# Three stages of a block become one stage walked by quarters of the sequence

## The reference

```python
h = x @ w_in + b_in                        # 1024 -> 9 groups of 512 columns
q_a, k_a, v_a, g_a, q_h, z_fwd, z_bwd, i_h, g_h = split(h)
# 8 heads of 64: tokens form 32 rows of 64; a token sees 8 rows x 16 columns around it
o_a = neighbourhood_attention(q_a, k_a, v_a, rpb) * silu(g_a)
# 4 heads of 128, forwards and backwards over the tokens
f = lb + (1 - lb) * sigmoid(z);  k = 1 - f
S_t = diag(f_t) S_{t-1} + k_t outer i_t;   o_t = S_t^T q_t
o_h = rms_norm(o_fwd + o_bwd) * gain * silu(g_h)
y = concat(o_a, o_h) @ w_out + b_out
return layer_norm(2**0.25 * x + y)
```

## Time and profile before

| | us |
|---|---|
| median of 3 runs (5614.87 to 5622.78) | 5621.27 |
| the profiled execution | 5620.12 |
| its span, first to last instruction | 5618.3 |
| block 3: turning and splitting x to the first projection matmul | 3613 to 3645 |
| block 3: projections | 3645 to 4437 |
| block 3: attention and recurrence | 4437 to 5343 |
| block 3: loading `w_out`, output projection and normalisation | 5343 to 5618 |

### The profile page before, as it was taken

The page is one execution under the profiler, slowest core; times in us unless marked ns, Lnnn a source line. Parts: engine busy times, 40 slices in busy tenths (PEclk is TensorE's granted clock), DMA queues, the critical chain, the costliest instruction groups (busy, mean ns, idle before and its releaser), DMA issues. The chain is left out here.

```text
span 5618.3 us, 61740 instructions
## 1 busy us (share of the span) xinstructions
PE 4567.0 (81%) x25432; PEld 3642.6 (65%) x25432; DVE 2463.2 (44%) x3040; ACT 1651.1 (29%) x2678; POOL 977.9 (17%) x529
## 2 busy tenths in 40 slices
PE   5999999988996999946766627799999866777767
PEld 2788888886775778824545515688888844555556
DVE  3488788625554303242222232211110177776733
ACT  2111111125554112212212224433331044545522
POOL 1111111112221111101101124211111032222123
PEclk9999999998997999968888858899999978888888
DMA  4111111232333111137766641322222243242132
GB/s 160 49 42 57 53 57 42 92 115 86 113 113 111 38 68 57 53 130 192 208 197 184 183 176 55 138 92 92 92 93 72 62 97 90 71 106 66 44 131 92
DMA packets 505640, 557.31 MB, mean 99 GB/s; under 512 B 45963, under 2 KB 396495, under 8 KB 498385
## 3 DMA queue, kind: packets, MB, share of 16 engines
q1 hardware_dynamic: 427409, 412.18, 24.7%
q10 hardware_dynamic: 77954, 141.19, 7.1%
HBM read 343.50 MB, written 193.00 MB: 95 GB/s over the span
## 5 line engine op out<-in xcount | busy, mean ns | idle before, releaser
L226 PE MATMUL ps<-hh,wsplit 128*128 128x512 f32 x2944 | 1173.8, 399 | 29.7 <-issue 25.1
L227 PE MATMUL ps<-hl,wsplit 128*128 128x512 f32 x2944 | 1164.9, 396 | 0.0
L228 PE MATMUL ps<-hh,wsplit 128*128 128x512 f32 x2944 | 1162.1, 395 | 0.0
L812 DVE SCALAR_TENSOR_TENSOR conv_acc<-conv_in,pcol,conv_acc 128x1024 f32<-128x1024 f32 x480 | 687.5, 1432 | 14.8
L226 PEld LDWEIGHTS ps<-hh,wsplit 128*128 128x128 f32 x2944 | 556.4, 189 | 161.6 <-issue 34.3
L218 POOL TENSOR_TENSOR wsplit<-wraw,wsplit 128x1024 fp32r<-128x1024 f32 x108 | 300.4, 2791 | 2023.0 <-ACT wsplit L213 2023.0
L227 PEld LDWEIGHTS ps<-hl,wsplit 128*128 128x128 f32 x2944 | 561.1, 191 | 131.5 <-issue 3.9
L228 PEld LDWEIGHTS ps<-hh,wsplit 128*128 128x128 f32 x2944 | 558.0, 190 | 127.8
L251 PE MATMUL ps<-wo,o_yh 128*128 128x512 f32 x1024 | 418.8, 409 | 79.6 <-DVE o_yl L2940 64.4
L252 PE MATMUL ps<-wo,o_yh 128*128 128x512 f32 x1024 | 413.3, 404 | 0.0
L253 PE MATMUL ps<-wo,o_yl 128*128 128x512 f32 x1024 | 411.5, 402 | 0.0
(11 more groups left out here) (305 smaller groups left out, 7039.1 us busy)
## 6 DMA issues: line engine op xcount, KB each, us to landing
wraw<-in_w_in SPq DMA_DIRECT2D x108, 512.0 KB, 3.9
sh<-hy_ak ACTq DMA_DIRECT2D x64, 512.0 KB, 4.7
o_ld<-y_tiles SPq DMA_DIRECT2D x48, 512.0 KB, 5.3
g_tiles<-b_ost SPq DMA_DIRECT2D x96, 256.0 KB, 2.4
wo_raw<-in_w_out SPq DMA_DIRECT2D x32, 512.0 KB, 5.0
x_rows<-o_x ACTq DMA_DIRECT2D x32, 512.0 KB, 2.6
hy_dec<-in_k_dec SPq DMA_DIRECT2D x64, 256.0 KB, 3.0
hy_kt<-sh SPq DMA_DIRECT2D x32, 512.0 KB, 6.7
```

The costliest lines, as they stand in the source:

```text
L226: e.matmul(p[:, :], wh, c.HH[tb][:, k, :], start=k == 0, stop=False)
L227: e.matmul(p[:, :], wh, c.HL[tb][:, k, :], start=False, stop=False)
L228: t = e.matmul(p[:, :], wl, c.HH[tb][:, k, :], start=False, stop=k == 7)
L812: e.scalar_tensor_tensor(v, a[:, h * 1024 + j:(h + 1) * 1024 + j], c.convw(j, ch), v, ALU.mult, ALU.add) \
```

## The change

One stage, `b3_*`, takes the place of the three.

- The tokens are walked in four quarters (`tb`) of 36 slots each, 144 in all. Each quarter turns and splits its own 512 tokens of x into one `L.HH`, `L.HL` (8x512 each), and loads and splits all 36 column tiles again: 144 loads and splits instead of 36, in a ring of four.
- Between slots the list places the recurrence, now in 64 units of 256 tokens whose inputs (k, b, f - b, q, values) stay in SBUF, and the attention.
- The recurrence's forward direction is finished in place. The backward direction runs from the last token, which is not known yet, so only its part within a chunk is made in the slots; its q factors and key-value products are stored to DRAM. After slot 144, 16 `chain` steps walk the states backwards, add them to the stored outputs, and normalise (`fin`, `fin2`, two heads at a time).
- An attention step now takes 4 rows by 16 columns of queries against up to 12 rows by 32 columns of keys: 384 keys, or 256 for the first and the last 4 rows. There are still 128 steps: 0, 16, 32 and 32 of them in the four quarters, and 48 after slot 144.
- The output projection begins at slot 163 of the same list, two slots to a tile, while attention steps are still placed until slot 178. Tiles go in the order `L.seq`. The bias is now added by GpSimd ahead of the statistics.
- Loads and stores are all issued by SP. Matmuls of projections and outputs share two PSUM banks, attention two, and products, key-value products and outputs of the recurrence one each; before, each stage had three to eight.
- Copies out of PSUM that ScalarE made before (queries and keys, L2146; turned keys, L2545) are made by VectorE.

The core of the diff (`b3_order` gives the places; the engine programs follow it):

```diff
-def p3_layout(c):
-    L = c.p3 = K()
...
-def mix_layout(c):
-    L = c.mx = K()
...
-def o3_layout(c):
-    L = c.o3 = K()
...
+    o = al(8192)
+    L.W, L.Wraw = view("w3", o, 4, 2048, r=True), view("w3_raw", o, 4, 2048)
+    o = al(8192)
+    L.HH, L.HL = view("h3_hi", o, 8, 512, r=True), view("h3_lo", o + 4096, 8, 512, r=True)
...
+    L.pb, L.ab = Banks(c, c.P[0:2]), Banks(c, c.P[2:4])
+    L.ra, L.rb, L.ob = Banks(c, c.P[5:6]), Banks(c, c.P[6:7]), Banks(c, c.P[7:8])
...
+def b3_order(L):
...
+    for tb in range(4):
+        for q in range(2):
+            pair("i", q, 28 + 2 * q)
+        for hd in range(4):
+            col("f", (hd, 0), 20 + hd)
+            col("f", (hd, 1), 24 + hd)
+            rq[tb, hd] = len(slots)
+            col("rq", hd, 16 + hd)
+            if tb < 3:
+                for kind, column in (("rg", 32), ("ag", 12), ("aq", 0), ("ak", 4)):
+                    col(kind, hd, column + hd)
...
+        if n >= 4:
+            after(last[n - 4], "ld", n)
+            before(last[n - 4] + 2, "split", n)
...
+    for n, (tb, hd, d, h) in enumerate(L.units):
+        r = rq[tb, hd]
+        e = r + (1, 2, 4, 5)[2 * d + h]
+        if d == 0 and h == 0:
+            before(r, "log", tb, hd)
+        before(e, "el", n)
+        after(e + 2, "prod", n)
+        after(e + 3, "state", n)
+        after(e + 4, "out", n)
...
+    def att_at(m, s):
+        v, a, j = L.steps[m]
+        after(s, "qk", m)
+        before(s + 1, "div", m)
+        after(s + 1, "turn", m)
+        after(s + 2, "val", m)
...
+        if g == 0:
+            s = 36 + 3 + 2 * k
+        elif g < 3:
+            s = 36 * (g + 1) + 3 + k
+        else:
+            s = 147 + k // 2 if g == 3 else 155 + 2 * k // 3
...
+    t0 = 144
+    for k in range(8):
+        after(t0 + k // 4, "wo", k)
+    for q, tb in enumerate(range(3, -1, -1)):
+        for hd in range(4):
+            n, s = 4 * q + hd, t0 + 1 + 4 * q + hd
+            after(s - 2 if n >= 2 else s, "ch_ld", n)
+            after(s - 2 if n in (2, 3) else s if n < 2 else t0 + 4 * q - 4 + (hd | 1) + 5, "fin_ld", n)
+            after(s + 1, "chain", n)
+            after(s + 2, "ch_o", n)
+            after(s + 3, "fin", n)
+            if n % 2:
+                after(s + 4, "fin2", n)
+    o0 = t0 + 19
+    L.seq = [15, 14] + list(range(9, -1, -1)) + [13, 12, 11, 10]
+    after(o0 - 2, "o_const")
+    for i in range(16):
+        s = o0 + 2 * i
+        after(s - 4, "y_ld", i)
+        before(s - 2, "y_split", i)
+        after(s, "o", i, 0)
+        after(s + 1, "o", i, 1)
+        after(s + 2, "o_end", i)
...
+def b3_sp(e, c):
...
+    def ld(n):
+        if n >= 4:
+            e.wait_ge(*L.done[L.last_unit[n - 4]])
+        col = tile_col(L, n)
+        e.dma_start(L.Wraw[:, n % 4, 1024:2048].rearrange("p (k n) -> p k n", k=8), w_in[:, col:col + 128].rearrange("(k p) n -> p k n", p=128)) \
+            .then_inc(*L.w_ld[n % 4].up(n))
...
+        for g in range(g0, g1 + 1):
+            for j in range(4):
+                src = c.VA[256 * g:256 * (g + 1), cs].rearrange("(r x) n -> r x n", x=64)[:, COL0[j]:COL0[j] + 32, :]
+                e.dma_start(L.V[:, s, 4 * (g - g0) + j, :], src).then_inc(*L.v_ld[s].up((v, g, j)))
...
+        elif k == "fin_ld":
+            n = s[1]
+            tb, hd = chain_unit(n)
+            sl = slice(512 * tb, 512 * tb + 512)
+            if n >= 4:
+                e.wait_ge(*L.ry_st[n % 4][n - 4])
...
+            e.dma_start(L.FO[n % 4], L.OD[hd][:, sl]).then_inc(*L.fo_ld[n % 4].up((n, "o")))
...
+def b3_pool(e, c):
...
+        elif k == "o" and s[2] == 1:
+            i = s[1]
+            e.wait_ge(*c.by_dve["out", 3, i, 1])
+            e.wait_ge(*L.c3_ld["ln_bias_3"])
+            e.tensor_tensor(L.XO[:, i % 3, :], L.XO[:, i % 3, :], L.bo, ALU.add).then_inc(*L.o_pool.up(("bias", i)))
+        elif k == "o_end":
+            i = s[1]
+            X = L.XO[:, i % 3, :]
+            e.wait_ge(*L.o_dve["n", i])
+            e.tensor_tensor(X, X, L.lg, ALU.mult).then_inc(*L.o_pool.up(("g", i)))
+            e.wait_ge(*L.o_pool["g", i])
+            e.tensor_tensor(X, X, L.lb, ALU.add).then_inc(*L.o_pool.up(("y", i)))
```

More of the change, by code:

```diff
@@ L2017, in b2_done @@
     return [L.o_pe[15, 1], L.o_act[("rs", 15), 1], c.by_dve["out", 2, 15, 1], L.o_pool[15], L.x2_st[0][14], L.x2_st[1][15]]
-def p3_layout(c):
-    L = c.p3 = K()
[L2024 to L2062, removed]
-    L.bound_a, L.bound_d = sig("bound_by_act"), sig("bound_by_dve")
-    L.f_out = [[dsig(f"forget_out{i}{j}") for j in range(3)] for i in range(2)]
-    L.f_log, L.f_step = sig("forget_log"), sig("forget_step")
@@ new lines, in tile_col, with levels, v3 @@
+def tile_col(L, n):
+    return L.tiles[n][2] * 128
+def levels(L, n):
+    tb, hd, d, h_ = L.units[n]
+    s, out = n % 2, []
+    for B, X in ((128, L.X[0]), (64, L.X[1]), (32, L.X[2])):
+        h = B // 2
+        qs, ks = (slice(h, B), slice(0, h)) if d == 0 else (slice(0, h), slice(h, B))
+        x = v3(X[:, s, :], B)
+        kd = x if B > 32 else v3(L.K32[d][:, s, :], 32)
+        out.append((B, x, kd, qs, ks))
+    return out
+def v3(v, m):
+    return v.rearrange("p (n x) -> p n x", x=m)
@@ new lines, in rq_unit, with chunk_unit, chain_state @@
+def rq_unit(L, tb, hd):
+    return next(u for u in L.order if u[0] == "col" and u[2:5] == (tb, "rq", hd))
+def chunk_unit(hd, at):
+    return first_of(at // 4, hd) + at % 4 // 2
+def chain_state(e, c, n, tb, hd):
+    L = c.b3
+    e.wait_ge(*L.ch_ld[n % 2][n, "kv"])
+    if n == 0:
+        e.wait_ge(*L.r_pe[63, "out", 1])
+        for q in L.qe_st:
+            e.wait_ge(*q.end())
+    for m in range(4):
+        j, k = 3 - m, 4 * (n // 4) + m
+        to, now, kv = chain_slot(L, hd, k + 1), chain_slot(L, hd, k), L.KC[:, n % 2, (3 - m) * 128:(4 - m) * 128]
+        if k == 0:
+            e.tensor_copy(to, kv).then_inc(*L.ch_dve.up((n, 1)))
+        else:
+            e.wait_ge(*state_in(L, n, m))
+            e.scalar_tensor_tensor(to, now, L.decb[:, 4 * tb + hd, j:j + 1], kv, ALU.mult, ALU.add).then_inc(*L.ch_dve.up((n, (m + 1) % 4)))
@@ new lines, in values @@
+    def values(m):
+        v, a, j = L.steps[m]
+        pr, groups, g0, g1 = L.visits[v]
+        w = L.avs.index((v, a))
+        bs, gs = step_bias(L, m)
+        e.wait_ge(*c.by_act["turn", m])
+        if j == 0 and w:
+            e.wait_ge(*c.by_dve["att_o", w - 1])
+        if m == L.first_step[v]:
+            e.wait_ge(*L.v_ld[v % 2][v, g1, 3])
+        for hh in range(2):
+            for i, g in enumerate(gs):
+                o = 256 * (w % 2) + 64 * j
+                t = e.matmul(c.P[4][64 * hh:64 * hh + 64, o:o + 64], L.V[:, v % 2, 4 * (g - g0) + j, 64 * hh:64 * hh + 64],
+                             L.PT[:, m % 3, 128 * i + 64 * hh:128 * i + 64 * hh + 64], start=i == 0, stop=i == len(gs) - 1)
+        t.then_inc(*L.a_pe.up(("val", m)))
@@ L2994, in o3_pe, with value_unit @@
                      L.WO, h, before if h == 0 else None).then_inc(*L.o_pe.up((i, h)))
+def value_unit(L, tb, hd, t):
+    return next(u for u in L.order if u[0] == "row" and u[2:] == (tb, "i", hd // 2, t))
 def sp_program(e, c):
```

1727 lines of the change are left out of this document (914 added, 813 removed).

## The result

The changed kernel takes 5640.57 us, median of 20 runs (5619.26 to 5662.54), against 5622.9 us of the kernel before in the same rounds: ratio 1.0033, 95% interval 1.0021 to 1.0044. It is a third of a per cent slower. The forecast was 5340 us.

A forecast was written before the change was run, and what follows sets the result against it. PE was taken to bound the slots: 3635 start + 1133 work + 113 order + 36 turning = 4917; plus 182 to the outputs and 240 for them, 5339, with 1.8 of profile excess 5341, said as 5340; range 5205 to 5550.

The forecast's parts named there:

- The slots: Block 3's projection slots with recurrence and attention beside them: PE is the bound, 1133 us of work, ending at 4917.
- their tenth: In the slots: engines walking in order cost 10% on top of PE's work, 113 us, between bounds of 7 and 317.
- the prediction's last rival: ScalarE's table loads in block 3: 2.66 us each with a drain, 57 more switches 152 us instead of 73; no chance of its own.
- the slower rival: In the slots: weight loads through SP's in-order list set the pace, slower than before from 10.6 us a slot, 5680; chance 0.08.
- the order bound for the slots: In the slots: the engines' order costs 317 us instead of 113, as in the mixed stage before, 5545 us; chance 0.22.
- all covered: From slots to outputs: waits nearly all hidden, slots pay 7, the part to 163 takes 150, outputs 228: 5190; chance 0.10.
- Slots 144 to 163: Between the projection slots and the outputs: 22 us of exposed load plus 160 for 16 slots, 182 us, bounds 134 and 214.
- exposed `w_out`: After the last projection slot: loading and splitting the output weights takes 28 us, of which 22 remain exposed.
- The output tiles: Output projection at the end: 114 us with attention, 111 without and a last chain of 15: 240 us, between 225 and 270.
- So tiles alone go at 11.65: Output tiles without attention: POOL's bias, statistics to gain, and gain and shift set 11.65 us a tile, 9.5 tiles 111 us.
- With attention ... I take 17.5 with waits: Output tiles beside attention: 16.7 us of PE work, 17.5 with waits, 6.5 tiles 114 us.
- The forecast's paragraph on the lock: In the slots: DVE and POOL block each other at a shared port, DVE gains 30 to 65 us, the sum unchanged.

## Why the prediction was wrong, by its own steps

**The slots: right.** 4917 forecast, 4916.5 measured; the first projection matmul at 3623.7 instead of 3635, so 11 us more went between them, and two misses cancel in the end point. Without the turning (13.3 to 13.9 us between quarters, 12 forecast) the quarters take 281, 292, 340 and 341 us, where the forecast's terms with their tenth give 275, 294, 337 and 337. The order cost of 10% holds in sum (1252.5 us for 1133 of work). It doesn't hold for each part: a step of the attention costs 2.3 us there, a quarter over its 1.85 and not a tenth. ACT loads its tables 190 times in block 3, exactly as counted, and a switch costs 1.31 us from the end of one operation to the start of the next (median of the kernel's 341), so the dearer price of the prediction's last rival is not paid here. ACT is busy 193 and 194 us in the last two quarters, where some 220 were reckoned, and DVE 220 and 227, where it was 200. ACT did stand 94.6 us for weight loads in all, but a slot came to 9.0 us, 9.5 in the last two quarters, below the 10.6 at which the slower rival would have decided. That rival, the order bound for the slots, and "all covered" all fell.

**Slots 144 to 163: the step that failed first.** "Between 7 and 12 us a slot I take 10: 160." Measured: (304.5 - 29.1) / 16 = 17.2 us, outside both bounds. The exposed `w_out` (22 us) was about right; the floor of the whole is 29.1. The mistake was the overlap: a slot was priced as one fin step with the attention beside it, 8.55 us, but the chain alone takes 8.2 us a slot and the attention alone 7.4, and the two add up (131 + 118.5) instead of overlapping. The store and load of the normalised rows were counted as the rows' median (2.4 + 3.4 us) without SP's place for them; they take 4.7 and some 4.5 to 5.0 here, and 25 us more come from SP's order. The forecast looked at DVE's work, "about 6 us in each" slot, and DVE was indeed busy 102 of 303 us.

**The output tiles: the larger error, 157 us.** "So tiles alone go at 11.65": POOL's own loop was walked, SP's list was not. In it stands the store of tile i-3, which waits for POOL, ahead of the load of tile i. With that one place changed, tiles take 12.0 us, so POOL's loop was about right and SP's, which stood above it, was missing. Only the last seven tiles pay it in full, since the first two had been loaded ahead (11.2 and 13.2 us): from 5455.0, the first matmul of the first tile alone, to the end of the last matmul the nine tiles take 140 us, where 9.5 at 11.65 were 111. The end behind them takes 22 us and not 15. "With attention ... I take 17.5 with waits": they took 36 ((5454.1 - 5237.7) / 6). From the first output matmul to 5455.0 that is 234 us and not 114, 120 us of the miss and the larger part; the order of load and normalisation takes 7 us a tile back (29.2), gain and shift off POOL 1.7. The forecast priced those tiles by PE's work, 11.2 + 3 x 1.85; the 117.7 us by which O falls without the attention are three times what that formula allows for 20 steps (20 x 1.85 = 37). What fills the rest of such a tile is not shown. The forecast's paragraph on the lock concluded that it changes nothing in the sum, and with the order mended no price of it can be told from nothing.

**The other side.** The rival that was to end slower sat in the slots. The one that happened, a tail of 48 attention steps and 16 chain steps with nothing large to hide them, was in the forecast's list only as a range of 134 to 214 us, which can't reach the other side.

**Left open.** What a step's 5 us in the tail consist of. PE's busy time in S is 115.6 us at a mean clock of 0.63. If all of it had run at the lower level, half the full clock, the full clock would have saved at most half of it; so by this estimate the clock explains at most 58 of the 275 us. The rest is waits from engine to engine and for transfers, which no run here took apart. DMA was half busy in S (0.50, 146 GB/s), and transfers do slow each other there: the stores of the normalised rows land in 4.7 us beside the attention and in 2.4 and 2.7 without it. For the eight pairs of heads that is some 2 us each, an estimate from these landings, and small beside 275. Issuing V from POOL was not tried.

## What to carry to other kernels

Work that fits into the shadow of a large stage costs little more than its PE time there (2.3 us a step against 1.85), and outside it cost more than twice that (5.5 us): count the steps that are left over when the large stage ends, and don't price them by PE's work, nor as hidden behind each other; here two kinds added up in full. Walk the DMA queue's list like an engine's: a store that waits for a result belongs behind every load that doesn't, and sixteen small loads are 14 us of list. When a change moves the time little, read the stretches one by one; here the slots' gain was lost again behind them, and edits of the order alone gave back a third of it (5641 to 5545 us of a miss of 300).

## What the runs showed of the hardware

- Issuing a 64 KB load of V with rows of 512 bytes takes SP 0.76 us mostly (14.27 us for 16 with some at 0.5 and one at 2.7), where a load of a tile takes 0.32 to 0.43. ACT's queue took 14.6 to 23.6 us for sixteen of them.
- ACT_TABLE_LOAD costs 1.31 us between the end of one ACT operation and the start of the next, 1.283 of it the load itself (median of 341 in the kernel after).
- A store of 256 KB lands in 4.7 us where V's small transfers stand ahead of it, and in 2.4 and 2.7 us where there are none.
- DVE's TENSOR_SCALAR with one SBUF tile as input is held until POOL's TENSOR_TENSOR ends, 2.53 and 2.32 us instead of 0.42. In the forecast I had reckoned only with operations with two SBUF inputs.
